# Moving the dilated cache copies: four more under way early, four at the very end

## The chip, the cores and the metric

The kernel runs on one core of one Trainium2 chip. The metric is the device time of one execution in microseconds; it is the median of several runs.

## The reference

One inference step of a one-layer decoder: 256 prompt tokens, and 8 samples with one new token each and a past of 2048. It is in float32 throughout. Cut to what matters here:

```python
hp = rms_norm(xp, norm_mix) * (1 + sc1_p) + sh1_p          # the same for the samples
qa, ka, va, qb, kb, vb = project_qkv(hp, w_in, positions)
oa = stick_breaking(qa, k_all, v_all)                       # samples: 16 pages of keys and values each
ob = dilated_attention(qb, ext_k, ext_v)                    # windows (128,1), (512,4), (2048,16)
x = x + g1 * merge_out(oa, ob, ...)
# PEER: 8 heads, top 16 of 128 x 128 experts, one row of u and of v per expert
s = einsum('thcd,hcnd->thcn', (h @ w_pq), sub_keys)
u = expert_u[expert]
act = gelu(einsum('thkd,td->thk', u, h))
out = einsum('thk,thkd->td', g * act, expert_v[expert])
# outputs, among others: the dilated caches, shifted by the new token
dil_k_sample = concatenate([cache_dil_k, kb_s], axis=1)[:, 1:]
dil_v_sample = concatenate([cache_dil_v, vb_s], axis=1)[:, 1:]
```

The last two lines are 8 samples x 2 caches x 2047 rows of 512 floats, which are copied from DRAM to DRAM: 67 MB of the 481 MB that the kernel moves.

## The kernel before

Every engine has its own program, written out by hand, and the programs meet at semaphores. In order of time: adaLN vectors and the q/k/v projection (weights in four slots of R, 1 MB each, loaded by GpSimd); the keys of the samples, page by page; then, from about 220 us, the stick-breaking attention of the prompt in four head pairs (`sticks_pair`), with the other adaLN vectors computed between its steps from 16 weight slots (`ada_slots`, L486, four slots for each pair); from about 320 us the dilated attention of the prompt beside the value pages and the dilated windows of the samples; from about 434 us the output projection; from about 496 us the PEER queries and scores (`query_group`, L841, and `score_group`), with eight more weights; and from about 569 us the experts.

The experts take half of the time. For each of 16 pairs of token block and head, GpSimd gathers 16 rows (L452), each 128 tokens x 2048 floats (u and v of one expert per token), into one of eight slots. VectorE takes the dot product with u (L1612, `dot_done`), ScalarE makes a diagonal of weights (L1155), and TensorE adds the v part (L890, `e_used`), which frees the slot. Row 0 to row 7 of the first head go into slots that the PEER weights and sub-keys leave; row 8 waits for the first `e_used`. The 8 samples follow with 8 more rows (L466, L905), so there are 264 rows.

SP's program issues what GpSimd's does not: the even chunks of the key and value pages (L286), the windows of the dilated values (L276), the outputs and the copies of the dilated caches. A copy is cut into pieces of a quarter of one sample's cache, 1.048 MB (`copy_piece(pair, odd, m, q)`, L321): `pair` and `odd` give the sample, `m` keys or values, `q` the quarter. There are 64. A piece waits for the one before it on its own semaphore `copied[2 * odd + m]`:

```python
if not (isinstance(pair, int) and isinstance(q, int) and pair + q == 0):
    sp.wait_ge(landed, pair * 64 + q * 16)
```

`copy_windows(pair, odd)` issues the eight pieces of one sample, keys and values in turn, so that two are under way. SP issues in order: whatever waits holds all that is behind it. Before the change 16 pieces stand in the phase of the keys, eight (pair 1, odd 0) between the value pages of the first and the second sample, and 40 behind the windows and the sub-keys. The second sample's value pages wait for `v_used`, which TensorE counts.

GpSimd's queue of transfers has the weights (L392), the odd chunks of the pages (L286), the windows of the dilated keys and all the gathers.

Of the kernel before, what the change touches and what calls it, by code (L numbers as in the profile page):

```python
# [26 lines left out]
NH = 8  # L27
# [12 lines left out]
TOPK = 16  # L40
# [12 lines left out]
HALF = 8  # L53
# [82 lines left out]
def build(nc, A):  # L136
    ctx = ExitStack()
    with ctx:
# [3 lines left out]
        def sem(name):  # L142
            return ctx.enter_context(nc.semaphore(name))
# [104 lines left out]
        s = {n: sem(n) for n in names}  # L248
# [23 lines left out]
        def window_rows(eng, to, b, slot, src, new, ready):  # L272

            rows = src[bass.ds(b, 1), :].rearrange("a (r n) -> (a r) n", n=DG)
            for g, n, sel in DILS:
                eng.dma_start(to[slot][0:n, g, :], rows[sel, :]).then_inc(ready[slot], 16)  # L276
            eng.dma_start(to[slot][DIL_ROWS:DIL_ROWS + 1, 1, :],
                          new[bass.ds(b, 1), (PAST - 1) * DG:]).then_inc(ready[slot], 16)
# [10 lines left out]
        def key_pages(eng, b, chunks, first=False):  # L289
            for c in chunks:  # L290
                page_chunk(eng, b, c, A["sb_k"], kv_ready, [] if first else [(s["k_used"], b * CPB + (c - CPB + 1))])

        def value_pages(eng, b, chunks, first=False):
            for c in chunks:
                page_chunk(eng, b, c, A["sb_v"], kv_ready,
                           [(s["k_used"], (NB - 1) * CPB + c + 1)] if first else [(s["v_used"], b * CPB + (c - CPB + 1))])
# [3 lines left out]
        @block.sync  # L300
        def _(sp):
            sp.dma_start(cT[:, :, :], A["cT"].rearrange("p (c n) -> p c n", c=KC)).then_inc(s["ct_in"], 16)
            sp.dma_start(ident, A["consts"][:, 0:P]).then_inc(s["id_in"], 16)
            for t in range(2):
                sp.dma_start(x[:, t, :], A["x"][t * P:(t + 1) * P, :]).then_inc(s["x_in"], 16)
            sp.dma_start(G[:, :, :], A["grp"].rearrange("p (v n) -> p v n", n=WC)).then_inc(s["g_in"], 16)
            sp.dma_start(gcols[:, :], A["gcols"]).then_inc(s["small_in"], 16)
            sp.dma_start(sbb[:, :], A["sb_bias"].to_broadcast([P, NH])).then_inc(s["small_in"], 16)
            sp.dma_start(pages[:, :], A["pages"]).then_inc(s["pages_in"], 16)
            sp.dma_start(const[:, P:], A["consts"][:, P:]).then_inc(s["c_in"], 16)  # L310
            sp.wait_ge(s["pages_in"], 16)

            def copy_piece(pair, odd, m, q):


                src, dst = ((A["dil_k"], A["dil_k_s"]), (A["dil_v"], A["dil_v_s"]))[m]
                n = (PAST - 1) * DG // 4
                landed = copied[2 * odd + m]
                if not (isinstance(pair, int) and isinstance(q, int) and pair + q == 0):
                    sp.wait_ge(landed, pair * 64 + q * 16)  # L320
                sp.dma_start(dst[bass.ds(pair * 2 + odd, 1), bass.ds(q * n, n)].rearrange("a (r n) -> (a r) n", r=P),  # L321
                             src[bass.ds(pair * 2 + odd, 1), bass.ds(q * n + DG, n)].rearrange("a (r n) -> (a r) n", r=P)
                             ).then_inc(landed, 16)

            def copy_windows(pair, odd):
                for q in range(4):
                    for m in range(2):
                        copy_piece(pair, odd, m, q)

            sp.wait_ge(s["w_used"], 4)
            key_pages(sp, 0, EVEN, first=True)
            for odd in range(2):
                copy_windows(0, odd)
            with sp.Fori(1, NB) as b:
                key_pages(sp, b, EVEN)

            sp.wait_ge(s["qkv_ev"], 5 * ROUNDS)
            sp.wait_ge(s["rot_done"], 6)  # L340
            for name, col in (("sb_k", KA), ("sb_v", VA), ("dil_k", KB_), ("dil_v", VB_)):
                for t in range(2):
                    sp.dma_start(A[name + "_p"][t * P:(t + 1) * P, :], QKV[:, t, col:col + DG]).then_inc(s["kv_out"], 16)
            for name, r, k in (("sb_k_n", 0, 2), ("sb_v_n", 2, 0)):
                for q in range(2):
                    sp.dma_start(A[name][:, q * WC:(q + 1) * WC],
                                 s4[(k + q) * QUAD:(k + q) * QUAD + NB, r, :]).then_inc(s["kv_out"], 16)

            value_pages(sp, 0, EVEN, first=True)
            copy_windows(1, 0)  # L350
            with sp.Fori(1, NB) as b:
                value_pages(sp, b, EVEN)

            sp.wait_ge(s["new_out"], 64)
            sp.wait_ge(s["dk_used"], NB)
            for b in range(NB):
                if b >= 6:
                    sp.wait_ge(s["vd_used"], b - 5)
                elif b >= 2:
                    sp.wait_ge(s["v_used"], (NB - 1) * CPB + 2 * (b - 1))  # L360
                window_rows(sp, DV, b, b % 6, A["dil_v"], A["dil_v_s"], dv_ready)
            sp.wait_ge(s["vd_used"], 3)
            sp.dma_start(subk, A["subk"].rearrange("p (g n) -> p g n", g=16)).then_inc(s["subk_in"], 16)
            for pair, odd in ((1, 1), (2, 0), (2, 1), (3, 0), (3, 1)):
                copy_windows(pair, odd)

            sp.wait_ge(s["h_ready"], 6)
            sp.dma_start(m_all[:, SHIFT2, :], A["norm_final"].to_broadcast([P, D])).then_inc(s["fin_in"], 16)
            for t in range(2):
                sp.wait_ge(s["y_ready"], t + 1)  # L370
                sp.dma_start(A["y_p"][t * P:(t + 1) * P, :], H[:, t, :]).then_inc(s["y_out"], 16)
            sp.wait_ge(s["y_ready"], 3)
            for k in range(QUADS):
                sp.dma_start(A["y_s"][:, k * WC:(k + 1) * WC], H4[k * QUAD:k * QUAD + NB, :]).then_inc(s["y_out"], 16)
            sp.wait_ge(s["kv_out"], 16 * 12)
            sp.wait_ge(s["new_out"], 64)
            for n in range(4):
                sp.wait_ge(copied[n], 16 * 4 * NB // 2)
            sp.wait_ge(s["y_out"], 16 * (2 + QUADS))
# [1358 lines left out]
```

## Time and profile before

| what | value |
|---|---|
| median of 3 runs | 1255.71 us (1253.91 to 1262.47) |
| the profiled execution | 1252.58 us, span 1250.9 us |
| busy: TensorE matmul / VectorE / ScalarE / GpSimd | 939.5 / 634.1 / 352.0 / 441.7 us |
| moved | 481.20 MB, mean 385 GB/s |
| GpSimd's transfers | 366.03 MB |
| SP's transfers | 114.66 MB |
| weights L392 / L397, 48 of 1024 KB | median 14.2 us from issue to landing |
| copies L321, 64 of 1023.5 KB | median 8.5 us from issue to landing |
| gathers L452, 256 | median 11.9 us from issue to landing |
| SP's idle time, largest cause | 648.0 us, waiting for VectorE's y (L371) |

The profile is that of one execution. Times in its rows count from the start of the span. "SPq" is the queue of SP's instructions; a row of it is the issue of a transfer and not the transfer. The landing of a transfer is when its semaphore was raised.

### The profile page before, as it was taken

How to read it: one execution, taken by the hardware profiler on the slowest of the kernel's cores; microseconds unless marked ns; L12 is line 12 of the kernel's file. 1: busy time of each engine (PE TensorE's matmuls, PEld its weight loads, DVE VectorE, ACT ScalarE, POOL GpSimd, SP SyncE). 2: the span in 40 equal slices, each digit the busy share in tenths (PEclk: the TensorE clock that was granted, in tenths of full speed). 3: DMA queues.
4: the chain of work that ended last, by engine and by line, in shares of the span. 5: the costliest groups of instructions: out<-in, count | busy, mean ns of one | idle time of the engine just before them, and what ended most of it. 6: DMA issues, size and time to landing. Idle time of an engine off the chain costs nothing.

```text
span 1250.9 us, 14521 instructions
## 1 busy us (share of the span) xinstructions
PE 939.5 (75%) x3666; PEld 428.5 (34%) x3666; DVE 634.1 (51%) x1606; ACT 352.0 (28%) x959; POOL 441.7 (35%) x497
## 2 busy tenths in 40 slices
PE   2796886566776897996687788877868777877774
PEld 1342332344421244883233233333323233322331
DVE  3200100233544434421577777777677777777755
ACT  1000001424311111212233333333334443344333
POOL 2102323102154100021244555445544555555551
PEclk9898887677889998998798998989988999999996
DMA  9999888977599999999999999999989999999996
GB/s 367 420 402 377 322 332 332 411 275 294 186 362 375 341 338 356 395 396 370 402 426 423 427 427 427 428 427 428 428 371 426 428 428 428 428 427 428 428 427 276
DMA packets 83707, 481.20 MB, mean 385 GB/s; under 512 B 11881, under 2 KB 12234, under 8 KB 42322
## 3 DMA queue, kind: packets, MB, share of 16 engines
q0 software_dynamic: 57216, 366.03, 71.5%
q1 hardware_dynamic: 26450, 114.66, 24.3%
q8 instruction: 21, 0.34, 0.1%
q14 instruction: 20, 0.16, 0.0%
HBM read 477.40 MB, written 70.32 MB: 438 GB/s over the span
## 4 chain that ended last, share of the span: by engine, by line
DMA 39%; PE 28%; issue 11%; DVE 7%; ACT 6%; SPq 3%; POOL 3%; POOLq 2%; DVEq 0%; ACTq 0%
DMA R<-in_uv,idst 26%; PE ps L890 10%; DMA out_dil_v_s<-in_dil_v 6%; PE ps L841 5%; DMA R<-in_sb_k 3%; PE ps L796 2%; POOL R L452 2%; PE ps L547 2%; DVE R L1612 2%; SPq L285 1%; DMA pages<-in_pages 1%; POOLq L285 1%; SPq L286 1%; DMA R<-in_uv,idec 1%; DMA R<-in_sb_v 1%
## 5 line engine op out<-in xcount | busy, mean ns | idle before, releaser
L890 PE MATMUL ps<-R,diag 128*128 128x512 f32 x1024 | 499.1, 638 | 153.4 <-ACT diag L1155 153.4
L452 POOL DMA_INDIRECT R<-in_uv,idst x256 | 313.6, 1225 | 357.3 <-PE ps L890 282.8
L1612 DVE CUSTOM_DVE_ANT_0 R<-R,H 128x1024 f32<-128x1024 f32 x264 | 319.3, 1224 | 193.3 <-DMA R<-in_uv,idst 182.3
L890 PEld LDWEIGHTS ps<-R,diag 128*128 128x128 f32 x1024 | 199.0, 202 | 453.5 <-ACT diag L1155 236.5
L1133 ACT ACTIVATE gel<-dots 128x2 f32<-128x2 f32 x132 | 26.8, 203 | 396.4 <-DVE dots L1612 396.4
L392 POOL DMA_DIRECT2D R<-in_wts x36 | 19.1, 530 | 242.9 <-PE ps L486 90.8
L547 PE MATMUL ps<-R,HT 128*128 128x512 f32 x192 | 92.0, 635 | 7.4 <-DMA R<-in_wts 7.4
L1155 ACT ACTIVATE diag<-const,wgt 128x128 f32<-128x128 f32 x256 | 88.7, 393 | 13.7 <-ACT wgt L1136 1.5
L671 PE MATMUL ps<-R,ast 128*32 128x512 f32 x256 | 57.3, 733 | 17.7 <-DMA R<-in_sb_v 16.5
L1136 ACT ACTIVATE wgt<-gel,gst 128x1 f32<-128x1 f32 x264 | 63.3, 287 | 4.3
L572 PE MATMUL ps<-R,Z 128*32 128x256 f32 x512 | 40.2, 465 | 31.9 <-DMA R<-in_sb_k 31.9
L841 PE MATMUL ps<-HT,R 128*128 128x264 f32 x256 | 60.1, 394 | 0.7 <-ACT HT L921 0.7
L547 PEld LDWEIGHTS ps<-R,HT 128*128 128x128 f32 x192 | 38.0, 203 | 56.9 <-issue 49.3
L286 POOL DMA_DIRECT2D R<-in_sb_k x64 | 34.5, 540 | 63.0 <-issue 51.7
L841 PEld LDWEIGHTS ps<-HT,R 128*128 128x128 f32 x256 | 49.2, 195 | 9.4 <-ACT HT L921 1.1
L286 POOL DMA_DIRECT2D R<-in_sb_v x64 | 34.6, 541 | 49.2 <-issue 40.6
L937 ACT ACTIVATE QKV<-ps 128x512 f32<-128x512 f32 x12 | 7.2, 597 | 155.4 <-PE ps L547 155.4
L486 PE MATMUL ps<-R,cT 128*32 128x256 f32 x384 | 32.7, 493 | 14.2 <-DMA R<-in_wts 14.2
L1285 DVE TENSOR_SCALAR Z<-ps,gcols 128x512 f32<-128x512 f32 x2 | 1.4, 748 | 78.4 <-PE ps L572 78.4
L572 PEld LDWEIGHTS ps<-R,Z 128*32 128x32 f32 x512 | 17.4, 126 | 52.3 <-DMA R<-in_sb_k 40.5
L1133 ACT ACT_TABLE_LOAD x24 | 30.8, 1283 | 1.0
L796 PE MATMUL ps<-R,HT 128*128 128x512 f32 x64 | 28.3, 595 | 0.7 <-DVE HT L1468 0.7
(271 smaller groups left out, 838.0 us busy)
## 6 DMA issues: line engine op xcount, KB each, us to landing
R<-in_wts POOLq DMA_DIRECT2D x48, 1024.0 KB, 14.2
out_dil_k_s<-in_dil_k SPq DMA_DIRECT2D x32, 1023.5 KB, 8.6
out_dil_v_s<-in_dil_v SPq DMA_DIRECT2D x32, 1023.5 KB, 8.5
R<-in_sb_k SPq DMA_DIRECT2D x64, 256.0 KB, 7.9
R<-in_sb_k POOLq DMA_DIRECT2D x64, 256.0 KB, 6.1
R<-in_sb_v POOLq DMA_DIRECT2D x64, 256.0 KB, 5.4
R<-in_sb_v SPq DMA_DIRECT2D x64, 256.0 KB, 6.7
R<-in_uv,idst POOLq DMA_INDIRECT x256, 11.9
```

The lines of the kernel that those rows point to most:

```text
L286: eng.dma_start(KV[c % KVS][:, g, :], cache[bass.ds(page, 1)].rearrange("a p n -> (a p) n")).then_inc(ready[c % KVS], 16)
L452: pool.indirect_dma_start(out=R[:, row_slot(k), :], out_offset=None, in_=A["uv"], in_offset=bass.IndirectOffsetOnAxis(ap=idst[:, par, k:k ...
L547: last = pe.matmul(ps[:, n, :], hT[:, 2 * k + c, t * P:(t + 1) * P], WA[k][:, c, half * 512:(half + 1) * 512], start=(k + c == 0), stop=(2 ...
L572: last = pe.matmul(ps[c * QUAD:(c + 1) * QUAD, bank, at:at + WC], qz[:, half, c, b, :], KV[cc][:, :, c * P:(c + 1) * P], start=(b == 0 and ...
L671: last = pe.matmul(quad(j, n % QUADS), ast[:, j, n, :], KV[c % KVS][:, g, :], start=(n < QUADS), stop=(n >= NPG - QUADS))
L796: last = pe.matmul(ps[:, n, :], hT[:, c, t * P:(t + 1) * P], WA[c // 2][:, c % 2, half * 512:(half + 1) * 512], start=(c == 0), stop=(c == ...
L841: last = pe.matmul(ps[:, j, 0:NTOK], W[k][:, c, j * P:(j + 1) * P], hT[:, c, :], start=(c == 0), stop=(c == KC - 1))
L890: last = pe.matmul(ps[:, banks + q, :], diag[:, k % 4, :], R[:, row_slot(k), D + q * 512:D + (q + 1) * 512], start=False, stop=False, skip ...
L1133: act.activation(gel[:, k:k + 2], dots[:, k:k + 2], ACT.Gelu_apprx_tanh).then_inc(s["gel_done"], 1)
L1136: last = act.activation(wgt[:, k + q:k + q + 1], gel[:, k + q:k + q + 1], ACT.Copy, scale=gst[:, k + q:k + q + 1])
L1155: act.activation(diag[:, k % 4, :], ident, ACT.Copy, scale=wgt[:, k:k + 1]).then_inc(s["diag_done"], 1)
L1612: dve.tensor_tensor_reduce(u, u, H[:, t, :], 1.0, 0.0, ALU.mult, ALU.add, dots[:, k:k + 1]).then_inc(s["dot_done"], 1)
```

## The change

Pair 1 is copied whole between the value pages of the first and the second sample, and quarter by quarter: for each quarter the four pieces of two samples' keys and values, which have four different semaphores. Pair 3 is copied in the same order, but its last quarter is taken out of there and put in front of the output of the second prompt block, behind a wait for 262 of the 264 dot products.

```diff
             value_pages(sp, 0, EVEN, first=True)
-            copy_windows(1, 0)
+            for q in range(4):
+                for odd in range(2):
+                    for m in range(2):
+                        copy_piece(1, odd, m, q)
             with sp.Fori(1, NB) as b:
                 value_pages(sp, b, EVEN)
...
-            for pair, odd in ((1, 1), (2, 0), (2, 1), (3, 0), (3, 1)):
-                copy_windows(pair, odd)
+            for odd in range(2):
+                copy_windows(2, odd)
+            for q in range(3):
+                for odd in range(2):
+                    for m in range(2):
+                        copy_piece(3, odd, m, q)
...
             for t in range(2):
+                if t == 1:
+                    sp.wait_ge(s["dot_done"], 2 * NH * TOPK + HALF - 2)
+                    for odd in range(2):
+                        for m in range(2):
+                            copy_piece(3, odd, m, 3)
                 sp.wait_ge(s["y_ready"], t + 1)
                 sp.dma_start(A["y_p"][t * P:(t + 1) * P, :], H[:, t, :]).then_inc(s["y_out"], 16)
```

SP between the value pages of the first sample and the loop over the others, before (`copied0` and `copied1` are the semaphores of keys and values of the even sample, `copied2` and `copied3` of the odd one):

```order
143 L286 DMA R<-in_sb_v 128x512
144 L321 DMA out_dil_k_s<-in_dil_k 16x16376 [waits copied0]
145 L321 DMA out_dil_v_s<-in_dil_v 16x16376 [waits copied1]
146 L321 DMA out_dil_k_s<-in_dil_k 16x16376 [waits copied0]
147 L321 DMA out_dil_v_s<-in_dil_v 16x16376 [waits copied1]
148 L321 DMA out_dil_k_s<-in_dil_k 16x16376 [waits copied0]
```

and after:

```order
143 L286 DMA R<-in_sb_v 128x512
144 L321 DMA out_dil_k_s<-in_dil_k 16x16376 [waits copied0]
145 L321 DMA out_dil_v_s<-in_dil_v 16x16376 [waits copied1]
146 L321 DMA out_dil_k_s<-in_dil_k 16x16376 [waits copied2]
147 L321 DMA out_dil_v_s<-in_dil_v 16x16376 [waits copied3]
148 L321 DMA out_dil_k_s<-in_dil_k 16x16376 [waits copied0]
```

The pattern goes on for 8 pieces before and for 16 after. A piece waited for the last but one; now it waits for the last but three.

SP at the end of its program, before:

```order
262 L321 DMA out_dil_k_s<-in_dil_k 16x16376 [waits copied2]
263 L321 DMA out_dil_v_s<-in_dil_v 16x16376 [waits copied3]
264 L368 DMA m_all<-in_norm_final 128x1024 [waits h_ready]
265 L371 DMA out_y_p<-H 128x1024 [waits y_ready] x2
266 L374 DMA out_y_s<-H 8x256 [waits y_ready]
```

and after:

```order
260 L375 DMA m_all<-in_norm_final 128x1024 [waits h_ready]
261 L383 DMA out_y_p<-H 128x1024 [waits y_ready]
262 L321 DMA out_dil_k_s<-in_dil_k 16x16376 [waits copied0,dot_done]
263 L321 DMA out_dil_v_s<-in_dil_v 16x16376 [waits copied1]
264 L321 DMA out_dil_k_s<-in_dil_k 16x16376 [waits copied2]
265 L321 DMA out_dil_v_s<-in_dil_v 16x16376 [waits copied3]
266 L383 DMA out_y_p<-H 128x1024 [waits y_ready]
267 L386 DMA out_y_s<-H 8x256 [waits y_ready]
```

Four pieces stand between the two blocks of y_prompt. The other engines' programs are the same.

## Rows read from the trace of the kernel before

**Rows 1.** The page, transfers in 40 slices of 31.27 us

```profile
GB/s 367 420 402 377 322 332 332 411 275 294 186 362 375 341 338 356 395 396 370 402 426 423 427 427 427 428 427 428 428 371 426 428 428 428 428 427 428 428 427 276
```

**Rows 2.** Windows: stretch, length, busy PE, PEld, DVE, ACT, POOL; PEclk, DMA share, GB/s

```profile
450.00:470.00 20.00, 19.16 (x66) 9.36 (x65) 9.05 (x18) 0.80 (x2) 0.00 (x0) 1.00 0.90 312
569.00:606.00 37.00, 21.59 (x38) 8.23 (x36) 7.94 (x19) 6.98 (x20) 6.55 (x7) 0.72 0.96 359
625.00:664.25 39.25, 30.69 (x66) 12.16 (x64) 29.03 (x77) 13.82 (x45) 19.30 (x17) 0.96 1.01 426
```

**Rows 3.** Timeline of GpSimd: issues of weights and of expert rows

```profile
238.15 0.53 POOL L392 DMA_DIRECT2D R<-in_wts  x1 [10.54 <-PE ps L486]
...
482.53 0.54 POOL L392 DMA_DIRECT2D R<-in_wts  x1 [63.22 <-PE ps L796]
...
487.69 0.53 POOL L392 DMA_DIRECT2D R<-in_wts  x1 [1.18 <-PE ps L796]
506.25 0.53 POOL L392 DMA_DIRECT2D R<-in_wts  x1 [18.03 <-PE ps L841]
514.64 0.53 POOL L392 DMA_DIRECT2D R<-in_wts  x1 [7.86 <-PE ps L841]
...
534.36 0.97 POOL L452 DMA_INDIRECT R<-in_uv,idst  x1 [0.30 <-issue]
535.63 1.14 POOL L452 DMA_INDIRECT R<-in_uv,idst  x1 [0.30 <-issue]
...
578.18 0.94 POOL L452 DMA_INDIRECT R<-in_uv,idst  x1 [7.86 <-PE ps L890]
```

**Rows 4.** Timeline of SP: start, length of the issue, what

```profile
230.90 0.59 SPq L321 DMA_DIRECT2D out_dil_k_s<-in_dil_k  x1
...
331.94 85.86 SPq L286 DMA_DIRECT2D R<-in_sb_v  x56
...
495.26 0.69 SPq L321 DMA_DIRECT2D out_dil_k_s<-in_dil_k  x1
...
561.49 0.67 SPq L321 DMA_DIRECT2D out_dil_k_s<-in_dil_k  x1
...
593.21 0.51 SPq L321 DMA_DIRECT2D out_dil_v_s<-in_dil_v  x1
```

**Rows 5.** The chain that ended last: start, length, what

```profile
523.63 7.14 PE ps L841 x32
...
532.01 7.14 PE ps L841 x32
...
569.39 37.27 DMA R<-in_uv,idst
...
633.24 12.65 DMA R<-in_uv,idst
```

**Rows 6.** Landings, issues at: 278-280; 482-489 (four); 506; 514; 533-537 (rows 0 to 2)

```profile
DMA to landing us min/median/max: 5.0/6.2/7.5
...
DMA to landing us min/median/max: 11.8/22.0/31.2
...
DMA to landing us min/median/max: 20.2/20.2/20.2
...
DMA to landing us min/median/max: 22.7/22.7/22.7
...
DMA to landing us min/median/max: 26.6/27.2/39.7
```

**Rows 7.** Timeline of TensorE beside the copies of the front

```profile
272.11 0.77 PE L624 MATMUL ps<-H,const 128*128 128x128 f32 x2 [6.24 <-DVE Z L1312]
...
275.79 3.04 PE L486 MATMUL ps<-R,cT 128*32 128x256 f32 x32
```

**Rows 8.** Timeline of the tail: VectorE's dot product 263 of 264, SP's last issues

```profile
1237.70 1.22 DVE L1612 CUSTOM_DVE_ANT_0 R<-R,H 128x1024 f32<-128x1024 f32 x1
...
1248.11 1.31 SPq L374 DMA_DIRECT2D out_y_s<-H  x4
```

## Prediction

> **What bounds the kernel now.** I read the strip of slices first [rows 1]. The transfers run at 427 or 428 GB/s from about slice 20 to slice 38, which is the whole expert phase, and well below that in two places: in slices 8 to 10 (about 250 to 344 us: 275, 294, 186 GB/s) and in slice 39. The window of one head of the experts shows 426 GB/s over 39.25 us [rows 2]. A head gathers 16 rows-of-experts of 128 x 2048 floats, 1.049 MB each, so a row costs 39.25 / 16 = 2.45 us, and 16 x 1.049 MB / 39.25 us is the 427 GB/s seen. TensorE is busy for 30.69 us of the 39.25, VectorE for 29.03: both have room. So from the time when this phase is in step until its end, only the number of rows left and the transfer rate count. The time can change only (a) by when the phase gets into step, (b) by delays before it, (c) in the tail.
>
> Getting into step is slow today. Row 8 of head 0 is issued at 578.18 [rows 3], but 569 to 606 us moves only 359 GB/s [rows 2], and part of it is dilated copies, which SP issues until 593.21 [rows 4]. The row issued at 569.39 takes 37.27 us to land [rows 5]. Row 23 is issued at 633.24 and lands 12.65 us later, at 645.9 [rows 5].
>
> **What the copies do to the other queue.** SP's transfers and GpSimd's go through two queues on the same engines. I take the time per 1.049 MB in GpSimd's queue from successive landings [rows 3, 6], each an issue plus its landing time. Weights issued from 482.53 to 487.69 land from 494.3 to 518.9: 8.2 us each, mostly with two copies under way. The weights issued at 506.25 and 514.64 land at 526.5 and 537.3: 10.9 us apart, with four copies under way for most of it. The expert rows issued at 534.36 and 535.63 land at 561.6 and 575.3: 13.7 us apart, across two copies that SP issues back to back from 561.49 [rows 4], while two more are under way. Beside no copy a weight lands in 5.0 us, of which 2.45 is the transfer, as above. So copies come first in practice, and four at once hold GpSimd's queue back more than two. The new order of the pieces has four under way all along, in both places where it is used. The copies themselves go at about 3.4 us a piece (1.048 MB at the 312 GB/s of 450 to 470 us, where there was next to nothing else [rows 2]).
>
> **The change, part by part.**
>
> First, 12 of the 40 pieces behind the windows are gone from there (8 to the front, 4 to the end). With 28 left, SP issues the first 16 as now and comes to pair 3 at 495.26 [rows 4], with two of pair 2 still under way. Those two and the 12 of pair 3 end at about 495.3 + 14 x 3.4 = 543 to 544 us, before the gathers matter. The expert phase then starts without copies. Row 8 still waits for TensorE, so it is issued at 578.18 at the earliest, lands 5.0 us later at 583.2, and row 23 lands 15 x 2.45 us after that, at 620.0 instead of 645.9. Gain: 26 us. TensorE needs 30.69 / 16 = 1.9 us per row, so it keeps ahead of 2.45.
>
> Second, the front. SP now issues 16 pieces from 230.90 instead of 8. They last until about 230.9 + 3 + 16 x 3.4 = 288 us (3 us from issue to movement, from the 5.0 - 2.45 above). SP itself loses nothing, since its next value page waits for TensorE until 331.94 [rows 4]. But four weights (A, B, C, D) are loaded by GpSimd beside them. The queue begins to move at 240.7 (238.15 [rows 3] + 5.0 - 2.45). TensorE wants C at 275.79 and D half-way through the same 3.04 us group, which ends at 278.83 [rows 7]. At 8.2 us each D lands at 273.5 and nothing slips. At 10.9 D lands at 284.3, and with 1.5 us of matmuls the group ends 7 us late. At 13.7 D is about half through when the copies end, lands at 289.3, and the group ends 12 us late. This stretch is a chain of short steps with nothing spare behind it, so a slip here moves all that follows. I take 12.3, the mean of the two stretches that held four copies: A 253, B 265.3 (its group may end as late as 272.11 [rows 7]), C 277.6, D 288.4: 11 us late.
>
> Third, the same in 504 to 544 us, where now two copies alternate with room between them. About 1.8 weights are still to come at 504 ((518.9 - 504) / 8.2). TensorE wants the fourth at 523.63 and the fifth at 532.01 [rows 5], and it is busy throughout, so any wait is added to the end. At 8.2: none. At 10.9 the fourth comes at 523.6 to 524.3, the fifth at 535.2, the sixth at 544.5 against 543.6: 4 us. At 12.3 the fourth comes 3 us late and the fifth 4 more: 7 us. At 13.7: 6 and 5, so 11 us.
>
> Fourth, the tail. The wait for 262 dot products is over at 1237.70 [rows 8], when one row is still on its way. Four copies of 1.048 MB take 9.8 us at 427 GB/s or 13.4 at 312, from about 1239.5, so they end at 1249.3 to 1252.9. The last block of y_prompt (0.524 MB, 1.2 us) and y_sample, which is issued at 1248.11 over 1.31 us, are queued behind them on SP. The end moves from 1250.9 to between 1251.5 and 1255: I take 2 us.
>
> The wait on the dot products holds only SP, which has nothing to issue there but y_prompt's second block. The split of pair 1 and pair 3 into quarters adds no issue: 64 pieces as before, 0.51 us each.
>
> Sum: -26 + 11 + 7 + 2 = -6 us. The profiled execution took 1252.58 us (span 1250.9), so 1246.6. The median of the three runs shown is 3.1 us above that execution, 0.25%, and by it the sum would be 1249.7. I predict 1247.
>
> A rule of the Trainium skill bears on the pace. DMA: Bandwidth & Descriptors, Queues, rings and completion order, says that each engine goes round the queues it has work for and drains a whole packet, typically 9 to 17 descriptors, before it switches. If so, a weight would need one turn or two and would cost, as my estimate from that page, some 5 us with any number of copies waiting, and the sum would be that of the light case below. The landings (8.2 to 13.7 us) do not agree with so large a packet. That the queues take turns at all speaks against a queue that is starved altogether.
>
> **Rivals.**
>
> Light contention. GpSimd's queue keeps the 8.2 us of today's copies, or up to about 11, because an engine alternates between the queues however many pieces wait. For it: the 8.2 us itself was read partly with four under way. Against it: 10.9 and 13.7. Time: -26 + 0 + 0 + 2 gives 1228.6, and at 10.9, -26 + 7 + 4 + 2 gives 1239.6.
>
> Heavy contention, which ends slower. The place is the same, the four weights of 238 to 288 us and the second to sixth of 504 to 544 us; the price is set by the pace. At 13.7 us the sum is -1. At 24 us B comes only when the copies end (288), so its group ends at 289.5 instead of by 272.11: 17 us, and C and D are then in time. The fourth weight comes at 544.3 instead of 523.63: 21 us. Sum: -26 + 17 + 21 + 2 = +14, so 1266.6. It decides from about 14.5 us per transfer on. For it: no row shows four copies under way for 40 us on end. Against it: the worst landing distance seen is 13.7.
>
> No effect. The 26 us are not had, since row 8 is not the start of a run in step: ScalarE's first weights wait for the query scores and a cold TensorE is slow (PEclk 0.72 in 569 to 606 [rows 2]). With half the gain and slips of 5 and 4 us the sum is -2, so 1250.6. For it: today's rows 8 to 15 wait for TensorE as well as for transfers. Against it: TensorE's 1.9 us per row leaves it ahead.
>
> **How the numbers follow.** Forecast (pace 11 to 14.5 us, -13 to +1): 0.42, own range 1239 to 1254. Light: 0.36, 1228 to 1240. No effect: 0.10, 1247 to 1258. Heavy: 0.12, 1256 to 1270. A measurement of this kernel tells about 1% from no change (its three runs span 0.7%), 12.5 us. Faster by more than that has the light case and a little of the forecast: 0.40. Slower has the heavy case: 0.12. Within 1%: 0.48. The range reaches from 1228, the light end, to 1261, half-way into the heavy case.
>
> **What would show it.** In the changed profile: 16 copies issued at 230.9 to about 276 us and over by 288; rates above 380 GB/s in slices 8 and 9; TensorE's group at 275.79 ending near 290, with a wait on weights that has no row today; scores ending 7 us later still; the row issued last before TensorE's first expert matmul landing in under 10 us instead of 37.27; heads still 39.25 us each; last copies landing about 1250 in today's time. I am wrong if the weights land in time in both places (then 1228 to 1240), if the first head still takes over 45 us, or if y_sample lands more than 5 us after its issue.

## The result and the profile after

The changed kernel takes 1267.83 us (median of 19 runs, 1261.17 to 1275.39) against 1255.77 for the kernel before (19 runs): the ratio is 1.0102, with a 95% interval of 1.0082 to 1.0122. It is about 1% slower. The forecast was 1247 us, range 1228 to 1261; the measured time lies outside the range. The profiled execution has a span of 1264.9 us, 14.0 more than before.

The strip of slices of the changed kernel answers to [rows 1]:

```profile
GB/s 366 419 384 392 305 344 351 397 355 319 193 339 375 382 316 313 391 355 204 296 427 427 427 427 428 427 427 427 428 380 427 428 427 427 428 427 428 427 427 349
```

The two slices after 250 us did fill up (355 and 319 where 275 and 294 stood), as intended. But slices 18 and 19 are now the emptiest of all behind slice 10 (204 and 296, where 370 and 402 stood): the copies behind the windows are over (the last one landed at 562.5 us), and the experts have not begun. More was moved early, and still everything after it came later.

The timeline of SP answers to [rows 4] and shows when the copies are issued:

```profile
229.70 0.59 SPq L321 DMA_DIRECT2D out_dil_k_s<-in_dil_k  x1
...
276.56 0.51 SPq L321 DMA_DIRECT2D out_dil_v_s<-in_dil_v  x1
...
449.14 0.35 SPq L366 DMA_DIRECT2D R<-in_subk  x1
...
549.13 0.51 SPq L321 DMA_DIRECT2D out_dil_v_s<-in_dil_v  x1
...
1247.52 0.52 SPq L321 DMA_DIRECT2D out_dil_k_s<-in_dil_k  x1
...
1257.92 1.62 SPq L386 DMA_DIRECT2D out_y_s<-H  x4
```

Next to it, GpSimd's timeline: the four weights that are loaded beside the copies of the front, and the third to fifth weight of the PEER queries (L404 is L392 of before).

```profile
238.34 0.54 POOL L404 DMA_DIRECT2D R<-in_wts  x1 [11.35 <-PE ps L498]
240.05 0.54 POOL L404 DMA_DIRECT2D R<-in_wts  x1 [1.17 <-PE ps L498]
249.26 0.53 POOL L404 DMA_DIRECT2D R<-in_wts  x1 [8.67 <-PE ps L498]
250.12 0.53 POOL L404 DMA_DIRECT2D R<-in_wts  x1 [0.33 <-issue]
...
501.29 0.53 POOL L404 DMA_DIRECT2D R<-in_wts  x1 [1.18 <-PE ps L808]
503.00 0.53 POOL L404 DMA_DIRECT2D R<-in_wts  x1 [1.18 <-PE ps L808]
522.38 0.53 POOL L404 DMA_DIRECT2D R<-in_wts  x1 [18.85 <-PE ps L853]
```

And the landings of these seven issues, in the same order, which answer to [rows 6]:

```profile
DMA to landing us min/median/max: 23.5/23.5/23.5
...
DMA to landing us min/median/max: 36.5/36.5/36.5
...
DMA to landing us min/median/max: 41.6/41.6/41.6
...
DMA to landing us min/median/max: 43.2/43.2/43.2
...
DMA to landing us min/median/max: 29.2/29.2/29.2
...
DMA to landing us min/median/max: 44.7/44.7/44.7
...
DMA to landing us min/median/max: 40.3/40.3/40.3
```

Adding each landing to its issue gives 261.8, 276.6, 290.9 and 293.3 us in front, and 530.5, 547.7 and 562.7 at the queries. While four copies are under way, one weight lands 14.3 to 17.2 us after the other. The fourth of the front came only 2.4 us after the third: by then the copies were over, the last of them having landed at 290.7.

TensorE's timeline answers to [rows 7] and to the first two of [rows 5]. The bracket is the idle time ahead of the row and what ended it.

```profile
276.56 1.93 PE L498 MATMUL ps<-R,cT 128*32 128x256 f32 x16 [11.62 <-DMA R<-in_wts]
...
290.90 1.94 PE L498 MATMUL ps<-R,cT 128*32 128x256 f32 x16 [9.02 <-DMA R<-in_wts]
293.34 1.89 PE L498 MATMUL ps<-R,cT 128*32 128x256 f32 x16 [0.51 <-DMA R<-in_wts]
...
547.70 9.03 PE L853 MATMUL ps<-HT,R 128*128 128x264 f32 x32 [7.95 <-DMA R<-in_wts]
562.68 10.06 PE L853 MATMUL ps<-HT,R 128*128 128x264 f32 x32 [4.69 <-DMA R<-in_wts]
...
607.92 12.26 PE L902 MATMUL ps<-R,diag 128*128 128x512 f32 x24 [1.86 <-ACT diag L1167]
```

Each of these rows but the last starts at the moment at which its weight landed; the last is TensorE's first matmul of the experts. The group that ended at 278.83 before ends after 295 now. In the chain that ended last, weights have taken a place that they did not have before:

```profile
250.12 43.18 DMA R<-in_wts
...
522.38 40.26 DMA R<-in_wts
...
642.69 12.65 DMA R<-in_uv,idst
```

The last of these is row 23 of the gathers. It lands at 655.3, while it landed at 645.9 before. TensorE began with the experts 33.6 us later than before, so most of that had been made good by then.

To see where the time goes, I divide the span of every kernel at rows of its timelines: the first copy of the front (SP), the issue of the sub-keys (SP, just ahead of the copies behind the windows), TensorE's first matmul of the PEER queries, its first matmul of the experts, the issue of the last expert row (GpSimd), and the end. Microseconds between them:

| kernel | front to sub-keys | to queries | queries and scores | experts | tail |
|---|---|---|---|---|---|
| before | 203.2 | 62.4 | 77.8 | 652.6 | 24.0 |
| changed | 219.4 | 62.7 | 96.1 | 628.9 | 28.1 |
| difference | +16.2 | +0.3 | +18.3 | -23.7 | +4.1 |

The first copy was itself issued 1.2 us earlier, and with that the sum is the 14.0 us of the span.

The queries and scores lost 18.3 us, of which TensorE's waits for the fourth and the fifth weight are 12.6. Most of the rest is slower work: the query matmuls (L841, L853 of the changed kernel) were busy for 60.1 us before and for 65.4 now. The granted clock (the column ahead of the last two) shows why. In a stretch with these matmuls before, and in one that begins with the end of the first of the two waits now, it was

```profile
540.00:575.00 35.00, 32.73 (x170) 26.64 (x169) 3.03 (x7) 9.72 (x30) 4.68 (x5) 1.00 0.99 391
```

```profile
547.00:573.00 26.00, 20.50 (x76) 16.69 (x76) 5.64 (x22) 2.35 (x10) 3.65 (x5) 0.79 0.96 372
```

so TensorE was granted its full 2.4 GHz throughout that stretch before, and only for a part of it now.

### The profile page after: what moved, and what is told of

Read it like the earlier page. It is cut to its first block, busy times and chain, and to the rows that moved or that the text cites. A ratio compares the mean times of both kernels' runs of the same rounds, so it can differ in the third digit from the quotient of the medians.

```text
span 1264.9 us, 14522 instructions
## 1 busy us (share of the span) xinstructions
PE 927.2 (73%) x3666; PEld 427.2 (34%) x3666; DVE 634.1 (50%) x1606; ACT 352.4 (28%) x959; POOL 442.2 (35%) x497
## 4 chain that ended last, share of the span: by engine, by line
DMA 46%; PE 24%; issue 10%; DVE 6%; ACT 6%; SPq 4%; POOL 2%; POOLq 1%; DVEq 0%; ACTq 0%
DMA R<-in_uv,idst 26%; PE ps L902 9%; DMA R<-in_wts 7%; DMA out_dil_v_s<-in_dil_v 6%; PE ps L853 3%; DMA R<-in_sb_k 3%; PE ps L808 2%; PE ps L559 2%; SPq L285 2%; POOL R L464 2%; DMA pages<-in_pages 1%; SPq L286 1%; DMA R<-in_sb_v 1%; ACT wgt L1148 1%; DVE R L1624 1%
## 5 line engine op out<-in xcount | busy, mean ns | idle before, releaser
L902 PE MATMUL ps<-R,diag 128*128 128x512 f32 x1024 | 487.6, 626 | 141.2 <-ACT diag L1167 141.2
L902 PEld LDWEIGHTS ps<-R,diag 128*128 128x128 f32 x1024 | 195.0, 198 | 433.7 <-ACT diag L1167 224.7
L404 POOL DMA_DIRECT2D R<-in_wts x36 | 19.2, 533 | 268.5 <-PE ps L498 106.2
L559 PE MATMUL ps<-R,HT 128*128 128x512 f32 x192 | 92.2, 636 | 7.7 <-DMA R<-in_wts 7.7
L853 PE MATMUL ps<-HT,R 128*128 128x264 f32 x256 | 65.4, 419 | 13.3 <-DMA R<-in_wts 12.6
L683 PE MATMUL ps<-R,ast 128*32 128x512 f32 x256 | 49.9, 722 | 20.3 <-DMA R<-in_sb_v 18.8
L853 PEld LDWEIGHTS ps<-HT,R 128*128 128x128 f32 x256 | 52.7, 209 | 24.0 <-DMA R<-in_wts 13.0
L498 PEld LDWEIGHTS ps<-R,cT 128*32 128x32 f32 x384 | 13.1, 133 | 50.5 <-DMA R<-in_wts 30.9
```

The costliest lines, as they stand in the source:

```text
L498: last = pe.matmul(ps[q * QUAD:(q + 1) * QUAD, bank, 0:WC], cT[:, 2 * k + c, :], WA[k][:, c, q * WC:(q + 1) * WC], start=(k + c == 0), sto ...
L559: last = pe.matmul(ps[:, n, :], hT[:, 2 * k + c, t * P:(t + 1) * P], WA[k][:, c, half * 512:(half + 1) * 512], start=(k + c == 0), stop=(2 ...
L683: last = pe.matmul(quad(j, n % QUADS), ast[:, j, n, :], KV[c % KVS][:, g, :], start=(n < QUADS), stop=(n >= NPG - QUADS))
L853: last = pe.matmul(ps[:, j, 0:NTOK], W[k][:, c, j * P:(j + 1) * P], hT[:, c, :], start=(c == 0), stop=(c == KC - 1))
L902: last = pe.matmul(ps[:, banks + q, :], diag[:, k % 4, :], R[:, row_slot(k), D + q * 512:D + (q + 1) * 512], start=False, stop=False, skip ...
```

## The experiments

My theory, N: it is the number of copies under way that slows GpSimd's queue. The rival, V: it is the volume copied beside the weights. Each kernel is the changed one except for what its diff shows, and is compared with the kernel before on the same chip.

### The front alone

```diff
-            for odd in range(2):
-                copy_windows(2, odd)
-            for q in range(3):
-                ...
+            for pair, odd in ((2, 0), (2, 1), (3, 0), (3, 1)):
+                copy_windows(pair, odd)
...
-                if t == 1:
-                    ...
```

> Only the front of the change: all 16 pieces of pair 1 early, four under way; behind the windows 32 pieces, two under way, as before; nothing held back for the end. My theory (N: it is the number of copies under way that slows GpSimd's queue, from about 8 us per 1 MB with two to 14 to 17 with four): the front slips by 15 to 16 us as in the changed kernel, the PEER scores take no longer than before (73 us from the first to the last L841-type group), the expert phase gains 20 to 24, no tail: 6 to 8 us faster than before (ratio 0.994). Rival V (volume: what counts is only how many bytes are copied beside the weights): the same here, since front volume and number go together, and nothing at the scores, where the volume is that of before.

Measured: ratio 0.9968 (0.9944 to 0.9992). The scores cost next to nothing, the expert phase gained 22.7 us, and there was no tail cost (all rows in the table below). The gain came out smaller than expected, because the stretch from the front to the sub-keys took 225.8 us and not 219. In that profile TensorE waited 21.6 us for weights in 240 to 325 us, about as in the changed kernel. From the first copy to the second sample's value pages it is 118.9 us, against 117.2 in the changed kernel and 101.0 before. So the front cost what it cost there, and 4.7 of the other 6.4 us came behind the pages, where no copy is under way; they are not explained.

### The front with two under way

```diff
-            for q in range(4):
-                for odd in range(2):
-                    for m in range(2):
-                        copy_piece(1, odd, m, q)
+            for odd in range(2):
+                copy_windows(1, odd)
```

> The changed kernel, but the 16 pieces of the front in the old order, one sample after the other, so two are under way. N: weights of the front land 8 to 9 us apart, the four adaLN vectors slip by 0 to 7 us instead of 15 (they are late only because the copies now last longer, until about 300), the rest as changed: 3 to 7 us slower than before instead of 13 (ratio about 1.004). V: the same bytes are copied beside the same weights, so the slip stays at about 15 and the whole at 1.010.

Measured: ratio 1.0012 (0.9984 to 1.0041), a little better than expected. The same 16 pieces, and TensorE's wait for weights in 240 to 325 us falls from the first row here to the second (waits of the changed kernel, then of this one: total, times, longest):

```profile
PE ps L498 <- DMA R<-in_wts: 21.1, 3, 11.6
```

```profile
PE ps L496 <- DMA R<-in_wts: 3.6, 4, 2.0
```

The stretch to the sub-keys is 207.3 us instead of 219.4. V falls for the front: the pieces are the same and 12.1 of the 16.2 us of slip are gone (in the two later kernels with this same front 7 to 8 us are, so the slip is never gone whole). The bytes copied in a given stretch are not quite the same, since the copies now end later (the last one lands at 298.8 instead of 290.7). What each queue moved in 250 to 285 us (q0 is GpSimd's, q1 SP's; packets, MB, share of the 16 engines' time) shows the size of both effects. The changed kernel:

```profile
q1 hardware_dynamic: 310, 10.09, 80.4%
q0 software_dynamic: 314, 2.31, 18.9%
```

and this one:

```profile
q1 hardware_dynamic: 258, 8.52, 59.0%
q0 software_dynamic: 734, 5.31, 38.6%
```

The copies moved a sixth less, and the weights more than twice as much. The scores still take 95.0 us, since pair 3 was left as it was.

### The queries with two under way

```diff
-            for q in range(3):
-                for odd in range(2):
+            for odd in range(2):
+                for q in range(3):
                     for m in range(2):
                         copy_piece(3, odd, m, q)
```

> The changed kernel, but the 12 pieces of pair 3 in the old order, two under way. N: the weights of the scores land 7 to 9 us apart again instead of 14 to 17, TensorE waits for none of them, and the 18 us that the scores lost are back: front +15, expert phase -24, tail +4, so 5 us faster than before (ratio 0.996). V: the same bytes beside the same weights, so 10 to 18 us of the loss stay (ratio 1.005 to 1.010).

Measured: ratio 1.0006 (0.9983 to 1.0029). The scores take 77.8 us again, to the tenth what they took before, and TensorE has no wait for weights there; the changed kernel has this one in 480 to 620 us:

```profile
PE ps L853 <- DMA R<-in_wts: 12.6, 2, 7.9
```

So exchanging two loops gives back 18.3 us, with the same 12 pieces in the same place, and V falls for the scores too. The whole is about 6 us short of the expected gain; again the stretch from the front to the sub-keys is longer (223.8 us).

### The last four held back, alone

```diff
-            for q in range(4):
-                ...
+            copy_windows(1, 0)
...
+            copy_windows(1, 1)
             for odd in range(2):
                 copy_windows(2, odd)
```

(Pair 3 is as in the kernel just above.)

> Only the end of the change: 8 pieces in front as before, 36 behind the windows with two under way, and the last four held back for the end. Both theories: no slip in front or at the scores, copies behind the windows end some 17 us earlier (about 587 instead of 602), so the expert phase gains 12 to 17 us, and the tail costs 4: 8 to 13 us faster than before (ratio 0.990 to 0.994). If holding back is what hurts, it is not faster than before.

Measured: ratio 0.9941 (0.9915 to 0.9966), 7.4 us, a little less than the 8 to 13 expected. The experts take 641.9 us against 652.6, the tail 28.7 against 24.0. Holding four pieces back is worth 10.7 in the experts and costs 4.7 in the tail.

### Both places with two under way, without and with the held-back pieces

The first has the front and the order behind it of the two kernels above, with all 32 pieces behind the windows; the second has 28 there and the last four at the end.

> Both gains without either cost: the 16 pieces of pair 1 in front, one sample after the other (two under way), 32 behind the windows, two under way, nothing held back. N, from the runs so far: front about 0 (front_two) to 3, scores 0, expert phase -22 to -23 (front_only), tail 0: 18 to 22 us faster than before (ratio 0.983 to 0.986). If the parts do not add up (the copies in front last until about 300 and reach into the next weights), it is no better than tail_only (0.994).

> The changed kernel with two pieces under way in both places and the last four held back as in the change. N: as the kernel above with 4 us more for the tail, since the expert phase cannot start earlier than it does there: 14 to 18 us faster than before (ratio 0.986 to 0.989). If the held-back pieces are worth something once the copies are out of the way, it is equal to or faster than the kernel above.

Measured: 0.9899 (0.9872 to 0.9927) and 0.9915 (0.9885 to 0.9945), both less than expected. The parts of the experts, the scores and the tail came as forecast. What is missing is in front, 212.6 and 211.4 us: the copies, slower each, last longer and reach the next pair of weights. TensorE waits in the first of the two:

```profile
PE ps L487 <- DMA R<-in_wts: 10.3, 3, 6.1
```

The held-back pieces bought nothing here: with 32 or with 28 pieces behind the windows the experts take 629.9 and 628.0 us. The landings of the last copy behind the windows fit that: it came 8.5 us before row 8 of the experts was issued with 32 pieces (573.9 against 582.4) and 29 us before with 28, while with the 40 pieces of the kernel before it came 23 us after (601.3 against 578.18). Once the copies were over some us before row 8, fewer of them gained nothing more.

### One, two and three under way in front

Three kernels with 16 pieces in front in the order of the change, 32 behind, none held back. Each piece waits in addition for the one that is `k` before it:

```diff
+            order = [(odd, m, q) for q in range(4) for odd in range(2) for m in range(2)]
+            for n, (odd, m, q) in enumerate(order):
+                if n >= k:
+                    o, w, r = order[n - k]
+                    sp.wait_ge(copied[2 * o + w], 64 + (r + 1) * 16)
+                copy_piece(1, odd, m, q)
```

> All 16 pieces in front in the order of the change, but each waits for the one before it, so one is under way; 32 behind, nothing held back. N: GpSimd's weights land 5 to 6 us apart beside the copies, each copy takes longer in turn (about 5 us a piece, so they last until about 310), and no weight is late by more than a few us. V (bytes): the same slip as with four, 15 us.

> The same with three under way. N: between two and four: weights of the front land 10 to 14 us apart, TensorE waits 5 to 14 us for them in 255 to 320 us. If it is a full queue that counts (an engine always finds another piece of the copy waiting), three is already as bad as four: 14 us apart and 20 us of waits.

> Two under way in the quarter order of the change. If the number under way is all, this is like two under way sample by sample: TensorE waits 4 to 11 us for weights in 240 to 325 us, against 0 with one and 22 with three and four. If the order of the pieces counts (neighbouring samples, four semaphores), it is nearer to 20.

TensorE's waits for weights in 240 to 325 us with two and with three under way; with one there is no such row at all:

```profile
PE ps L491 <- DMA R<-in_wts: 6.5, 3, 3.2
```

```profile
PE ps L491 <- DMA R<-in_wts: 22.8, 3, 12.2
```

With the 21.6 us of four under way (the first experiment) that makes 0, 6.5, 22.8 and 21.6 us. It is no straight line: three is as bad as four, which was the second of the two cases stated before the run, and not my theory's "between two and four". Waits alone could mislead here, since a late weight costs nothing until TensorE wants it. What GpSimd's queue moved in 250 to 285 us depends on that much less: 5.60 MB with one under way, 5.70 with two, 2.45 with three, and 2.31 with four in the changed kernel. I read it as a full queue: from three on an engine always finds another piece waiting. The traces have no row for the queue of one engine, so that reading stays an inference. The order of the pieces, quarter by quarter or sample by sample, matters little (with two under way 6.5 us here, against 3.6, 10.3 and 10.4 in the kernels above). At the queries number and order were only exchanged together. Each of these three kernels was executed once: 1237.39, 1237.32 and 1246.89 us with one, two and three under way.

One at a time is not free either. In that kernel's chain the copies follow one another, 5.5 to 8.3 us each where about 5 had been expected, and the last ones hold SP when its value pages are due:

```profile
230.57 6.75 DMA out_dil_k_s<-in_dil_k
237.34 5.89 DMA out_dil_v_s<-in_dil_v
...
332.40 6.20 DMA out_dil_k_s<-in_dil_k
338.62 0.51 SPq L321
343.89 9.60 DMA R<-in_sb_v
```

SP wanted the pages at 331.94 [rows 4]. The stretch to the sub-keys is 211.2 us.

> The kernel with one piece under way in front and 32 behind, once more and timed. No weight was waited for, but the sixteenth piece was issued at 338.6 and SP's value pages, which wanted to start at 331.9, behind it, so 8 us went there. N: 12 to 15 us faster than before (ratio 0.988 to 0.990), the same as two under way with their 10 us of waits for weights.

Measured: ratio 0.9892 (0.9863 to 0.9922), as expected. In this profile the stretch to the sub-keys is 205.0 us, so the 8 us of the profile above do not come in full in every execution. The pages still went out right behind the sixteenth piece (332.70 and 334.28 us), 106.1 us after the first copy; it was 109.6 above and 101.0 before the change.

### Twelve in front, one at a time

The front ends before the pages are due. One kernel holds four back, the other has 36 behind the windows and holds none. The diff is against the kernel above with `k` = 1.

```diff
-            order = [(odd, m, q) for q in range(4) for odd in range(2) for m in range(2)]
+            order = [(odd, m, q) for q in range(3) for odd in range(2) for m in range(2)]
...
+            for odd in range(2):
+                for m in range(2):
+                    copy_piece(1, odd, m, 3)
             for odd in range(2):
                 copy_windows(2, odd)
```

> One under way in front but only 12 pieces there, 32 behind the windows with two under way, and four held back for the end as in the change. The front copies end before 325, so SP is free at 331.9 and no weight is late: front 0, scores 0, expert phase -22, tail +4: 17 to 19 us faster than before (ratio 0.985 to 0.987). If the last four at the end are not worth 4 us, it equals the kernel with 16 in front.

> The same with 36 behind the windows and nothing held back. tail_only had 36 behind, and its expert phase took 12 us longer than with 32 or 28; the tail is 4 us shorter: 8 to 12 us faster than before (ratio 0.990 to 0.993), so holding back pays 5 to 8 us here.

Measured: 0.9886 (0.9862 to 0.9909), a little less than expected, and 0.9921 (0.9899 to 0.9943), as expected. The first has the lowest ratio of the study, but that does not make it the best: its interval overlaps with those of all the kernels with 16 in front and one or two under way, and by medians the one with one under way was as fast (1234.11 us against 1235.25, beside 1249.40 for the kernel before). Its strip of slices shows what was wanted from the start, a fuller front and no hole ahead of the experts:

```profile
GB/s 366 423 412 383 279 335 351 367 319 365 252 365 388 354 323 350 371 404 390 423 427 427 428 427 428 427 427 428 427 371 426 428 427 428 427 427 428 427 428 344
```

Held back or not is 628.7 against 639.8 us of experts and 28.5 against 24.0 of tail, 6.6 us for holding back, inside the 5 to 8 expected. The intervals of the two ratios just overlap, so the runs' times do not show this by themselves.

All kernels, divided at the same rows as above, with one more: "front to value pages" ends where SP issues the second sample's value pages, and is a part of "front to sub-keys". In all kernels but dose2 a "2" means one sample after the other, and that has up to four pieces under way for some us at each change of sample.

| kernel | pieces in front, under way | behind | end | front to value pages | front to sub-keys | queries and scores | experts | tail | ratio |
|---|---|---|---|---|---|---|---|---|---|
| before | 8, 2 | 40, 2 | 0 | 101.0 | 203.2 | 77.8 | 652.6 | 24.0 | 1 |
| changed | 16, 4 | 28, 2 then 4 | 4 | 117.2 | 219.4 | 96.1 | 628.9 | 28.1 | 1.0102 |
| front_only | 16, 4 | 32, 2 | 0 | 118.9 | 225.8 | 78.6 | 629.9 | 24.0 | 0.9968 |
| front_two | 16, 2 | 28, 2 then 4 | 4 | 101.3 | 207.3 | 95.0 | 627.0 | 28.0 | 1.0012 |
| back_two | 16, 4 | 28, 2 | 4 | 118.9 | 223.8 | 77.8 | 630.4 | 28.3 | 1.0006 |
| tail_only | 8, 2 | 36, 2 | 4 | 100.9 | 205.5 | 78.0 | 641.9 | 28.7 | 0.9941 |
| best | 16, 2 | 32, 2 | 0 | 109.2 | 212.6 | 78.7 | 629.9 | 23.9 | 0.9899 |
| both_two | 16, 2 | 28, 2 | 4 | 108.7 | 211.4 | 78.7 | 628.0 | 28.7 | 0.9915 |
| dose1 | 16, 1 | 32, 2 | 0 | 109.6 | 211.2 | 78.5 | 628.7 | 24.0 | not timed |
| dose1_timed | the same |  |  | 106.1 | 205.0 | 78.1 | 631.2 | 23.9 | 0.9892 |
| dose2 | 16, 2 | 32, 2 | 0 | 107.2 | 212.3 | 78.1 | 629.2 | 23.9 | not timed |
| dose3 | 16, 3 | 32, 2 | 0 | 119.3 | 222.8 | 78.0 | 630.0 | 24.0 | not timed |
| front_12 | 12, 1 | 32, 2 | 4 | 98.9 | 202.0 | 78.2 | 628.7 | 28.5 | 0.9886 |
| front_12_all | 12, 1 | 36, 2 | 0 | 100.5 | 202.1 | 77.7 | 639.8 | 24.0 | 0.9921 |

The columns of the scores, the experts and the tail repeat within 3.5 us wherever the pieces are the same. The stretch from the front to the sub-keys does not: it differs by up to 6.4 us between kernels with the same front. Up to the value pages the kernels fall into groups: 98.9 to 101.0 us with 8 pieces or 12, 101.3 to 109.6 with 16 and one or two under way, 117.2 to 119.3 with 16 and three or four. The remainder, where no copy but a last one is under way, takes 98.9 to 106.9 us and does not follow the number of copies. These are single profiles, so a difference of a few us between two of them says little.

## Why the prediction was wrong

**What bounds the kernel: right.** A row of experts takes 2.47 to 2.49 us in every kernel whose time was measured (issues of rows 24 to 250, on average), against the 2.45 of the prediction, and the experts' phase depends only on when it gets into step.

**The gain of the experts, -26: right.** Measured -23.7. Row 8 was issued at 611.36, when TensorE had begun at 607.92; the row issued last before that, at 602.99, landed in 5.6 us, as the prediction said it should (under 10). The rival "no effect" is out: front_only, with nothing else changed behind it, gained 22.7.

**The slips, +11 and +7: wrong, and this is the step that failed.** They were 16.2 and 18.3. The mechanism was the one named, GpSimd's queue held back where four copies are under way, and both places were named; the term mis-sized is the time per weight. I took 12.3 us, the mean of 10.9 and 13.7, as the pace of "the two stretches that held four copies". With four all along it was 14.3 to 17.2. Neither stretch held four for as much as half of its time, and the prediction's "for most of it" is a misreading. The copies that SP issued around them in the kernel before were these (with 561.49 of [rows 4] between the last two):

```profile
523.45 0.51 SPq L321 DMA_DIRECT2D out_dil_k_s<-in_dil_k  x1
526.64 0.51 SPq L321 DMA_DIRECT2D out_dil_v_s<-in_dil_v  x1
527.20 0.60 SPq L321 DMA_DIRECT2D out_dil_k_s<-in_dil_k  x1
527.84 1.10 SPq L321 DMA_DIRECT2D out_dil_v_s<-in_dil_v  x1
...
557.70 0.51 SPq L321 DMA_DIRECT2D out_dil_k_s<-in_dil_k  x1
...
562.20 0.59 SPq L321 DMA_DIRECT2D out_dil_v_s<-in_dil_v  x1
```

The one issued at 523.45 landed 9.1 us later, at 532.6, and the one at 557.70 8.0 us later, at 565.7. So four were under way for 4.8 of the 10.9 us and for 3.5 of the 13.7, and two or three for the rest. Both rows were mixtures, and their mean could at best be a lower bound for four under way all along. Nor is the 13.7 a steady pace: the distance of the landings just before it is 2.0 us (559.6 to 561.6), and the one behind it 5.4 (575.3 to 580.7).

A second error sits in the same step. I let the first weight of the front move from 240.7 and land at 253. That is where it landed beside two copies (252.3 in the kernel before). It landed at 261.8, 23.5 us after its issue, where it had taken 14.2. The second then came at 276.6, past the 272.11 that the prediction itself gives as the latest harmless time. At the queries the step from 10.9 to 17.2 us per weight made TensorE wait for the fourth and the fifth weight, 12.6 us, as the prediction says of its slower cases. The lower clock behind these waits cost about 5 us more, a term that the prediction does not have.

**The tail, +2: too small.** Measured +4.1. Between 1254 and 1260 us the chip moved 349 GB/s at a DMA share of 1.08, nearer to the 312 of the copies alone than to 427, and the end came at the upper end of the range given (1251.5 to 1255). One of the prediction's signs of being wrong looks at this place: the span ended 7.0 us after y_sample was issued at 1257.92, where it had ended 2.8 after.

**The weighing.** The rival "heavy contention" gave 1266.6 us at a pace of 24 us and said that it decides from about 14.5 on. The pace was 14.3 to 17.2 and the time 1267.83. So this rival had the place and the direction right. That its number came out within 2 us is partly luck: at 24 us per weight only B would have been late in front, while in fact B, C and D all were, and the queries lost 18.3 us where it had 21. It had a chance of 0.12, on the ground that the worst distance seen was 13.7. That was no ground: nothing before had held four under way for 40 us, as the same paragraph says, and both rows that held four for a part of their time lay above the 8.2 of mostly two.

**The rule of the Trainium skill** (DMA: Bandwidth & Descriptors, Queues, rings and completion order): the queues take turns packet by packet. That GpSimd's queue was never starved agrees with it: its weights went on landing at 14.3 to 17.2 us beside four copies. The estimate of 5 us per weight "with any number of copies waiting", which I drew from its typical packet, holds only for one under way, where the first four weights of the front landed 4.5 to 5.0 us apart on average. With two it was 6.7 to 8.2, and the turns that the trace shows with four are much shorter than that packet (last section).

## What to carry to other kernels

A background transfer into a hole in the bandwidth is not free because bytes are spare. What counted here is how many of its pieces were queued when an urgent load came: with one or two TensorE waited at most 10.4 us in all for the weights of the front, with three or four over 20. So throttle the filler by a wait on its own earlier piece, give it as few in flight as still end in time, and check that the engine that issues it is free when its own next load is due. When pricing such a case from a trace, count from issues and landings how many transfers were under way during each row. If no row holds the state to be priced all along, the rows are bounds on one side, and the range has to go well past them. The size of a piece was never varied here; whether smaller pieces would do as well as fewer is open.

## What the runs showed of the hardware

The number of DRAM copies under way on SP's queue changes the service of GpSimd's queue, and not in proportion. For the weights of the front, with the same 16 pieces (16.8 MB) copied:

| copies under way | first weight, issue to landing | first to second landing | GpSimd's queue in 250 to 285 us | TensorE's waits for weights |
|---|---|---|---|---|
| 1 | 7.8 to 8.3 us | 4.8 to 5.2 us | 5.6 to 5.7 MB | 0 |
| 2 | 12.2 to 14.3 us | 4.6 to 7.5 us | 5.0 to 5.7 MB | 3.6 to 10.4 us |
| 3 | 21.1 us | 15.0 us | 2.45 MB | 22.8 us |
| 4 | 22.7 to 23.5 us | 14.0 to 14.8 us | 2.3 to 3.2 MB | 20.5 to 21.6 us |

The first weight waits longer with each copy that is under way when it is issued; the distance of the landings behind it jumps between two and three.

With four under way the packets of the trace show who gets what. In 240 to 290 us of the changed kernel, when weights were waiting in GpSimd's queue all along, that queue has 430 packets of 8 KB and SP's has 210 of 65.5 KB: two for one. A weight is eight such 8 KB packets on each of the 16 engines, so it lasts for about four packets of a copy. They took 0.31 and 2.93 us (medians), and 4 x (2.93 + 2 x 0.31) = 14.2 us, an estimate, is what the landings show.

Copies alone did not reach the 427 GB/s of the gathers: 312 GB/s in 450 to 470 us, mostly with two under way [rows 2]. With weights beside four copies the mixture moved 366 GB/s at a DMA share of 1.01:

```profile
229.00:292.00 63.00, 27.43 (x180) 16.89 (x184) 15.44 (x34) 20.96 (x24) 3.19 (x6) 0.64 1.01 366
```

So the engines were counted busy throughout and still moved a seventh less than in the experts' phase (426 at the same share [rows 2]).
